# Hybrid streaming encoder layer: the mixing loop's tile in another order on all engines, and the pair diagonal by a product and a head mask

## What is computed

```python
def sink_attention(q, k, v, dist, valid, sinks):
    s = jnp.einsum('bnqkgd,bnskd->bnkgqs', q, k).astype(jnp.float32) * (HEAD_DIM ** -0.5)
    s = s - slopes[None, None, :, :, None, None] * dist[None, :, None, None, :, :]
    ...
    p = jax.nn.softmax(jnp.concatenate([s, sink], axis=-1), axis=-1)[..., :-1]
    return jnp.einsum('bnkgqs,bnskd->bnqkgd', p.astype(v.dtype), v)

def hgrn_block(S, q, k, i, logf):
    b = jnp.cumsum(logf, axis=1)
    decay = jnp.exp(jnp.where(causal, b[:, :, None] - b[:, None, :], -jnp.inf))
    a = jnp.sum(q[:, :, None] * k[:, None] * decay, axis=-1)
    o = jnp.einsum('btsh,bshv->bthv', a, i) + jnp.einsum('bthk,bhkv->bthv', q * jnp.exp(b), S)
    b_last = b[:, -1]
    kd = k * jnp.exp(b_last[:, None] - b)
    S_new = jnp.exp(b_last)[..., None] * S + jnp.einsum('bshk,bshv->bhkv', kd, i)
    return S_new, o

    ob = rmsnorm(ob, o_norm) * jax.nn.silu(gb)
    mix = jnp.concatenate([oa, ob], axis=-1)
    x = x + g1 * jnp.dot(mix, w_out)
    h2 = rmsnorm(x, ln2) * (1 + sc2) + sh2
```

## Time and profile before

| | |
|---|---|
| time, median of 3 runs (lowest to highest) | 1498.12 us (1497.85 to 1501.41) |
| the profiled execution's own time | 1499.57 us |
| its span in the trace | 1497.8 us |
| mean granted TensorE clock | 0.885 of full speed |
| PE busy | 1248.5 us, 83% of the span |
| DVE busy | 727.3 us, 49% |
| ACT busy | 547.4 us, 37% |
| POOL busy | 356.7 us, 24% |

### The profile page before, as it was taken

One profiled execution on the slowest core, in us unless ns is written; L12 is line 12 of the kernel. 1 busy time (PEld: TensorE's weight loads), 2 busy tenths in 40 slices (PEclk: granted clock), 3 DMA queues, 4 the chain that ended last, 5 costly groups with the idle time before them and its releaser, 6 DMA issues. The chain is left out here.

```text
span 1497.8 us, 21761 instructions
## 1 busy us (share of the span) xinstructions
PE 1248.5 (83%) x7145; PEld 1032.7 (69%) x7146; DVE 727.3 (49%) x1062; ACT 547.4 (37%) x921; POOL 356.7 (24%) x411
## 2 busy tenths in 40 slices
PE   4789999995285888888888882699999999969964
PEld 1668889884254777677777671588888787858853
DVE  2554313423343545644554526555338665865662
ACT  2454313322222334423433410444316544654540
POOL 1001100223202323332232200223143234323313
PEclk8899999998557978888889875799999999989988
DMA  9527653312806322212211105648757979888874
GB/s 344 209 78 267 228 199 104 106 43 75 223 1 177 98 68 95 81 44 67 96 44 57 38 32 216 219 154 266 241 167 246 357 252 303 282 304 260 267 279 84
DMA packets 119143, 249.89 MB, mean 167 GB/s; under 512 B 17681, under 2 KB 47121, under 8 KB 116002
## 3 DMA queue, kind: packets, MB, share of 16 engines
q1 hardware_dynamic: 106978, 204.92, 39.3%
q0 software_dynamic: 12096, 44.05, 11.2%
HBM read 205.02 MB, written 43.93 MB: 166 GB/s over the span
## 5 line engine op out<-in xcount | busy, mean ns | idle before, releaser
L2044 PE MATMUL psum<-e_w_h,e_x_h 128*128 128x512 f32 x432 | 174.3, 404 | 30.8 <-DVE w_gu L2157 23.9
L2045 PE MATMUL psum<-w_gu,e_x_h 128*128 x432 | 171.6, 397 | 0.0
L2046 PE MATMUL psum<-e_w_h,e_x_l 128*128 128x512 f32 x432 | 171.4, 397 | 0.0
L1991 POOL DMA_INDIRECT out<-e_work,e_to x26 | 87.9, 3379 | 302.9 <-DVE e_work L2145 302.9
L2157 DVE TENSOR_TENSOR w_gu<-w_gu,e_w_h 128x1024 f32 x128 | 146.7, 1218 | 21.4 <-ACT e_w_h L2098 21.4
L2098 ACT ACTIVATE e_w_h<-w_gu 128x1024 fp32r x128 | 123.0, 1048 | 53.6 <-issue 31.9
L2044 PEld LDWEIGHTS psum<-e_w_h,e_x_h 128*128 128x128 f32 x432 | 83.3, 193 | 49.2 <-DVE w_gu L2157 24.4
L465 PE MATMUL psum<-p_w_h,p_h_h 128*128 128x512 f32 (+1 forms) x288 | 106.4, 370 | 1.6 <-DVE p_h_l L620 1.6
L466 PE MATMUL psum<-p_w_l,p_h_h 128*128 128x512 f32 (+1 forms) x288 | 105.5, 366 | 0.0
L467 PE MATMUL psum<-p_w_h,p_h_l 128*128 128x512 f32 (+1 forms) x288 | 105.4, 366 | 0.0
L2046 PEld LDWEIGHTS psum<-e_w_h,e_x_l 128*128 128x128 f32 x432 | 83.1, 192 | 17.9
(11 more groups left out here) (362 smaller groups left out, 2647.9 us busy)
## 6 DMA issues: line engine op xcount, KB each, us to landing
w_gu<-in_w_e_gate SPq DMA_DIRECT2D x16, 2048.0 KB, 15.2
w_gu<-in_w_e_up SPq DMA_DIRECT2D x16, 2048.0 KB, 19.0
w_dn<-in_w_e_down SPq DMA_DIRECT2D x16, 2048.0 KB, 15.0
p_stage<-in_w_ada SPq DMA_DIRECT2D x24, 1024.0 KB, 6.6
p_w_raw<-in_w_in SPq DMA_DIRECT2D x5, 2048.0 KB, 9.2
m_feat<-feat_d SPq DMA_DIRECT2D x8, 1024.0 KB, 6.6
m_tok<-tok_d SPq DMA_DIRECT2D x8, 896.0 KB, 8.2
tok_d<-p_tok SPq DMA_DIRECT2D x27, 256.0 KB, 2.0
```

Of the source, the lines that this page charges most:

```text
L1991: pool.indirect_dma_start(out=d["y"], out_offset=bass.IndirectOffsetOnAxis(ap=to_now[1 - par][:, 0:1], axis=0), in_=y_s[:, 1 - par, :], in ...
L2044: pe.matmul(psum[:, j, :], x_h[:, k, :], wh, start=(k == 0), stop=False)
L2045: pe.matmul(psum[:, j, :], x_h[:, k, :], wl, start=False, stop=False)
L2046: last = pe.matmul(psum[:, j, :], x_l[:, k, :], wh, start=False, stop=(k == KC - 1))
```

## The change

- **The diagonal**: POOL multiplies K and Q element by element into a new tile `prod`, and PE sums it over the channels of each head by four matmuls against a mask of two columns (`head_cols`), which leave eight numbers a row in PSUM. DVE spreads these over the identity. The eight full products of 128 columns go.
- **The attention turn**: `o_a` is turned in the output bank W0, behind a wait for DVE's first step of `residual` (`x1_ready`), in place of S0.
- **The next query turn**: queries and keys of tile t + 1 are turned behind the last `fill` of tile t, ahead of the state update, and ACT copies them there (`keep_qk`). The diagonal of tile t + 1 stands between the state's part and the attention turn.
- **The order within a tile**: `scores` of the first half stands ahead of the first `fill`, two `fill`s stand between level 0 and level 1, the scores of the second half come ahead of level 3, and their `tops` on DVE ahead of `place` of level 3. On DVE `heads_normed` (the norm of group B's output), `normed` and `rest` of the second half go from where they were to behind a `place`. On ACT `norm` goes from the tile's end to behind `exp_b` of the next tile and uses `h2_t` as its scratch, and the copy of the attention turn goes ahead of the norm factors `o_rs`. On POOL the product stands ahead of the moves of `v`, then `k_d`, the third gap and `weigh`.

```diff
+        prod, head_cols = sb("prod", [P, QW]), sb("head_cols", [P, 2])
...
                 make_gap(t, 0)
                 make_gap(t, 1)
                 if t >= 1:
-                    pool.wait_ge(s["kd_turned"], t)
-                pool.tensor_tensor(f4(k_d[:, :]), f4(fts(t, EK)), last_bc(f4(fts(t, CUM))[:, :, P - 1:P], P), ALU.add).then_inc(s["kgap_ready"], 1)
-                if t >= 1:
-                    weigh(t - 1)
-                make_gap(t, 2)
+                    pool.wait_ge(s["diag_mm"], t)
+                else:
+                    pool.wait_ge(s["eps_made"], 1)
+                pool.tensor_tensor(prod[:, :], fts(t, KB), fts(t, QB), ALU.mult).then_inc(s["prod_ready"], 1)
                 pool.wait_ge(tok_loaded[t % 2], 16 * (t // 2 + 1))
                 if t >= 1:
                     pool.wait_ge(s["pv_mm"], 2 * t)
                     alone(pool)
...
-                else:
-                    pool.wait_ge(s["eps_made"], 1)
                 pool.tensor_copy(v_sb[:, 1, :], toks(t, TOK_V, KW)).then_inc(s["v_ready"], 1)
+                if t >= 1:
+                    pool.wait_ge(s["kd_turned"], t)
+                pool.tensor_tensor(f4(k_d[:, :]), f4(fts(t, EK)), last_bc(f4(fts(t, CUM))[:, :, P - 1:P], P), ALU.add).then_inc(s["kgap_ready"], 1)
+                make_gap(t, 2)
+                if t >= 1:
+                    weigh(t - 1)
...
-            for t in range(TP):
+
+            def turn_qk(t):
                 pe.wait_ge(tok_loaded[t % 2], 16 * (t // 2 + 1))
                 if t:
-                    pe.wait_ge(s["mixa_ready"], t)
+                    pe.wait_ge(s["pt_ready"], 2 * t)
...
                 last.then_inc(s["qk_turned"], 1)
-                pe.wait_ge(feat_loaded[t % 2], 16 * (t // 2 + 1))
-                pe.wait_ge(s["state_ready"], t + 1)
-                for h in range(8):
-                    r = slice((h % 2) * HD, (h % 2 + 1) * HD)
-                    c = slice((h // 2) * P, (h // 2 + 1) * P)
-                    last = pe.matmul(psum[:, M0 + h % 2, c], fts(t, KB)[r, c], fts(t, QB)[r, c], start=True, stop=True)
-                    if h >= 6:
-                        last.then_inc(s["diag_mm"], 1)
+
+            def diagonal(t):
+                pe.wait_ge(s["prod_ready"], t + 1)
+                for c in range(4):
+                    last = pe.matmul(psum[:, M0, 2 * c:2 * c + 2], prod[:, c * P:(c + 1) * P], head_cols[:, :], start=True, stop=True)
+                last.then_inc(s["diag_mm"], 1)
+
+            turn_qk(0)
+            diagonal(0)
+            for t in range(TP):
+                scores(t, 0)
                 fill(t, 0)
-                scores(t, 0)
                 level(t, 0)
+                fill(t, 1)
+                fill(t, 2)
+                level(t, 1)
+                turn_probs(t, 0)
+                fill(t, 3)
                 if t:
                     turn_ob(t - 1)
-                fill(t, 1)
-                level(t, 1)
+                level(t, 2)
                 if t:
                     pe.wait_ge(s["mixb_ready"], t)
                     turn_h2(t - 1)
-                fill(t, 2)
-                level(t, 2)
-                turn_probs(t, 0)
+                scores(t, 1)
+                level(t, 3)
                 if t:
                     logits(t - 1)
-                fill(t, 3)
+                fill(t, 4)
                 values(t, 0)
-                scores(t, 1)
-                level(t, 3)
-                fill(t, 4)
                 level(t, 4)
+                turn_probs(t, 1)
                 fill(t, 5)
-                turn_probs(t, 1)
                 level(t, 5)
                 fill(t, 6)
                 values(t, 1)
...
                 fill(t, 7)
+                if t + 1 < TP:
+                    turn_qk(t + 1)
...
+                pe.wait_ge(s["state_ready"], t + 1)
...
-                turn4(S0, o_a[:, :, :, :].rearrange("p g k d -> p (g k d)"), s["oa_turned"])
+                if t + 1 < TP:
+                    diagonal(t + 1)
+                pe.wait_ge(s["x1_ready"], t + 1)
+                turn4(W0, o_a[:, :, :, :].rearrange("p g k d -> p (g k d)"), s["oa_turned"])
...
-                a(score[:, :, :].rearrange("p g n -> p (g n)"), x2[:, u % 2, :], ACT.Square, accum_out=ss[:, :]).then_inc(s["squared"], 1)
+                if u < NU - 2:
+                    if u:
+                        act.wait_ge(s["logit_mm"], u)
+                        alone(act)
+                    out = h2_t[:, :, :].rearrange("p k r -> p (k r)")
+                else:
+                    out = score[:, :, :].rearrange("p g n -> p (g n)")
+                a(out, x2[:, u % 2, :], ACT.Square, accum_out=ss[:, :]).then_inc(s["squared"], 1)
...
+            def keep_qk(t):
...
-                gap_exp(t, 0)
+
+            act.wait_ge(s["eps_made"], 1)
+            high(0, 0)
+            high(0, 1)
+            gap_exp(0, 0)
+            gap_exp(0, 1)
+            keep_qk(0)
+            for t in range(TP):
...
-                gap_exp(t, 1)
+                if t:
+                    norm(t - 1)
+                gap_exp(t, 2)
+                act.wait_ge(s["kgap_ready"], t + 1)
+                a(k_d[:, :], k_d[:, :], ACT.Exp).then_inc(s["kexp_ready"], 1)
+                gap_exp(t, 3)
+                probs(t, 0)
+                copy_probs(t, 0)
+                gap_exp(t, 4)
                 if t:
                     keep_ob(t - 1)
                     high(t, 1)
-                act.wait_ge(s["kgap_ready"], t + 1)
-                a(k_d[:, :], k_d[:, :], ACT.Exp).then_inc(s["kexp_ready"], 1)
...
-                gap_exp(t, 3)
-                copy_probs(t, 0)
-                gap_exp(t, 4)
                 gap_exp(t, 5)
                 probs(t, 1)
                 gap_exp(t, 6)
                 copy_probs(t, 1)
+                if t + 1 < TP:
+                    gap_exp(t + 1, 0)
+                    gap_exp(t + 1, 1)
                 act.wait_ge(s["kd_turned"], t + 1)
                 a(kd_tok[:, :], psum[:, OB, :], ACT.Copy).then_inc(s["kdt_ready"], 1)
+                if t + 1 < TP:
+                    keep_qk(t + 1)
                 act.wait_ge(s["ob_mm"], t * 2 + 2)
                 a(o_sq.rearrange("p (a c) d -> p a (c d)", a=2), psum[:, OA:OA + 2, 0:4 * HD], ACT.Square).then_inc(s["osq_ready"], 1)
+                act.wait_ge(s["oa_turned"], t + 1)
+                a(mixed(t + 1, 0), f4(psum[:, W0, :]), ACT.Copy).then_inc(s["mixa_ready"], 1)
+                high(t + 1, 0)
                 act.wait_ge(s["oss_ready"], t + 1)
                 olink = Chain(act, s["o_rs"], 2 * t)
                 olink(a(o_rs[:, :], o_ss[:, :], ACT.Ln, scale=1.0 / HD, bias=eps[:, :]))
                 olink(a(o_rs[:, :], o_rs[:, :], ACT.Exp, scale=-0.5))
-                act.wait_ge(s["oa_turned"], t + 1)
-                a(mixed(t + 1, 0), f4(psum[:, S0, :]), ACT.Copy).then_inc(s["mixa_ready"], 1)
-                high(t + 1, 0)
-                norm(t)
+            norm(TP - 1)
...
+            for par in range(2):
+                dve.memset(head_cols[0:HD, par:par + 1], 1.0 - par)
+                dve.memset(head_cols[HD:P, par:par + 1], float(par))
...
-                decayed(t, 0)
-                dve.wait_ge(s["diag_mm"], t * 2 + 2)
-                if t:
-                    dve.wait_ge(s["ob_mm"], 2 * t)
-                    alone(dve)
-                dve.tensor_tensor(pair[:, :, :, :].rearrange("p a h t -> p (a h) t"), psum[:, M0:M0 + 2, :].rearrange("p a (h t) -> p (a h) t", t=P),
-                                  bc(ident[:, :], 1, 8), ALU.mult).then_inc(s["pair_clear"], 1)
-                decayed(t, 1)
-                if t:
-                    normed(t - 1)
-                tops(t, 0)
-                if t:
...
+            def heads_normed(t):
...
+            for t in range(TP):
+                decayed(t, 0)
+                dve.wait_ge(s["diag_mm"], t + 1)
+                if t:
+                    dve.wait_ge(s["ob_mm"], 2 * t)
+                    alone(dve)
+                dve.tensor_tensor(pair[:, :, :, :], last_bc(psum[:, M0, 0:8].rearrange("p (c a) -> p a c", a=2).unsqueeze(3), P),
+                                  bc(bc(ident[:, :], 1, 4), 1, 2), ALU.mult).then_inc(s["pair_clear"], 1)
+                decayed(t, 1)
+                tops(t, 0)
+                dve.wait_ge(s["pair_clear"], t + 1)
+                place(t, 0)
+                if t:
+                    heads_normed(t - 1)
+                decayed(t, 2)
+                place(t, 1)
+                if t:
+                    normed(t - 1)
+                denominators(t, 0)
+                decayed(t, 3)
+                place(t, 2)
+                if t:
+                    rest(t, 1)
+                decayed(t, 4)
+                tops(t, 1)
+                place(t, 3)
+                if t:
+                    keep_logits(t - 1)
...
+                place(t, 6)
+                residual(t)
+                dve.wait_ge(s["ob_mm"], 2 * t + 2)
```

(62 more changed lines are left out.)

11 lines of the change are left out of this document (added).

## The result

The changed kernel takes **1437.9 us** (median of four runs, 1432.15 to 1438.73) against 1497.98 for the kernel before: ratio 0.9592, 95% interval 0.9557 to 0.9627. It is faster, as forecast, by two thirds of the forecast 93 us, and 1.9 us above the range's upper end of 1436. The profiled execution took 1437.97 us, 61.6 less than that of before. Nearly all of it lies in the mixing loop: behind the last attention turn stand 619.2 us, before 620.3.

A forecast was written before the change was run, and what follows sets the result against it. PE was taken to bound the kernel through its work, its waits and a slow clock behind them. Gains of 10.9, 1.5, 11.4, 15.6, 3.1, 2.8 and 49.6 less 2.1 made 92.8 us: forecast 1405 us, range 1392 to 1436.

The forecast's parts named there:

- clock term: Tiles 1 to 7: without pauses of 2 us the slow clock behind them goes, gaining 49.6 us (35.7 to 57.5).
- The 13 busy microseconds at 1.00: Busy stretch at 636 to 649, logits and turns included, that kept full clock; cited against falls in busy work.
- The diagonal: Sixteen 128-column records become eight of two columns, 0.85 us in all; gain 0.35 us a tile, 2.8 us.
- The third rival: Slower: clock falls in the busy stretch between tiles without 512-column matmuls and stays low through fills; about 1607 us, chance 0.03.
- the second rival: Clock follows the kind of work, not the waits, and keeps falling; no clock gain, 1455 us, chance 0.05.
- The waits: PE's pauses in the mixing loop mostly go; 40.4 us gained with the tail's 1.5, three small waits remaining a tile.
- The tail: Behind the last tile, where no scores follow: wait falls from 3.69 to about 2.2 us, gaining 1.5.
- ahead of level 1: PE's wait for `place` of level 0: 0.4 us a tile left of 14.2 us in all, gaining 11.4.
- the first exponentials: PE's first probability turn waits for ACT: a new wait of 0.3 us a tile, costing 2.1 us.
- the first fill: Turn of the tile: PE waits 0.6 us for `rest` behind the scores, 15.1 us before, gaining 10.9.
- Moved waits: Other waits shifted by the new order, such as `x1_ready`, `ob_mm`, `norm` and the feature load: each costs zero.
- Tile 0: First tile's idle time of 6.0 us, 2.15 counted elsewhere; the other 3.8 become 0.7, gaining 3.1 us.

The follow-up runs named there:

- e7: Changed kernel with diagonal mask and logits both widened to 128 columns, and tile 0's first fill ahead of its diagonal and scores: 1405.1 us.
- e3: Changed kernel with the two-column diagonal mask read 64 times over, 128 columns a matmul, at the same place: 1421.7 us.
- e11: e7 with the two-column diagonal mask put back at its place, nothing else changed: 1432.2 us.
- e8: e7 with level 1 ahead of the third fill instead of behind it, so PE waits there again: 1426.8 us.
- e9: Changed kernel with the two-column diagonal mask read 16 times over, 32 columns a matmul: 1419.7 us.
- e12: e10 with the last fill's final matmul ahead of the pairs instead of behind three quarters of them: 1416.2 us.
- e10: e11 with the two-column diagonal moved ahead of the state update's matmuls and the last fill's six matmuls spread around it: 1431.2 us.

## Why the prediction was wrong, point by point

**The step that failed is the clock term**, "if pauses of 2 us go, what followed them goes", with "I found no fall in busy work". It was 49.6 us. Busy time of the loop fell by 12.9 in all, diagonal included, where the sum had 49.6 + 2.8 = 52.4. Tiles 1 to 7, on which the term was worked out, were 19.2 less busy (317.48 to 298.26), and tile 0 was 6.3 more. In e7, which but for the first fill of tile 0 keeps the changed kernel's order, and which has no falls in tiles 1 to 7, it fell by 354.4 - 302.4 = 52.0. So the size of the term was about right and its condition was not: the falls behind the waits went, and new ones came in busy work, at the turns. The 13 busy microseconds at 1.00 with the logits among them were no evidence against such falls: in e3 the clock goes right behind the logits in five tiles and stays in two.

**The diagonal** was costed by its records alone: 0.85 us forecast, 0.92 at 2.4 GHz in the second turn. The hidden price is 27.1 us on a kernel without other falls (e11 less e7) and about 16 in the changed kernel itself (after less e3, where the logits then lose the clock): the narrow diagonal thins out a stretch that was poor already. The third rival named this stretch, with the two-column diagonal in it. Its condition came true; its extent, low through all fills, did not: the clock was back after some 7 to 14 us, among the fills, so the cost was nowhere near 152. It was given 0.03, and no case stood for a part of it. The time lies between the forecast and the second rival (1455, no clock term at all), which was right in part too: the kind of work does make the clock fall, but waits do as well (e8).

**The waits** came out better than forecast: 47.8 us in the loop against 38.9 (40.4 less the tail's 1.5). With the clock at 1.00 they are what the sum said: 0.4 ahead of level 1, 0.3 at the first exponentials, 0.2 instead of 0.6 at the first fill, all in e7. In the changed kernel the slow work ahead of them hides them, worth 6.0 us (e7 less after), so this part of the gain is no merit of the new order. The tail gave 0.65 of its 1.5: 3.04 are left.

**Moved waits** at zero: right, no other line waits in the loop. **Tile 0**: its waits went, but it did not get the 3.1 us. Its busy time rose from 36.9 to 43.3 us; 1.7 of that is the next tile's query turn and diagonal, which now stand in it, and for the rest its turn, diagonal and scores started at the low clock and stayed there for 15.5 us from the first record (9.8 in e3, 15.8 in e11, 3.2 in e7, which has both the wide mask and the early fill).

Adding up: 47.8 of waits and 12.9 of busy time are 60.7 in the loop, with 1.1 behind it 61.8 of the 61.9 by which the span is shorter. That e7 lands on the 1405 of the forecast is no merit of the forecast: it needed edits that the change doesn't have.

## What to carry to other kernels

Do not cost a matmul by its time alone: where the clock follows what PE streams, saving columns in a stretch that is already thin can cost far more than it saves (here 16 to 27 us against a forecast 2.8), and reading the same operand several times over can be a gain. When waits are taken out, look at the busy stretches that are left and read the granted clock in each, on several tiles; one stretch at 1.00 proves nothing for the next tile (e3). A forecast that rests on the clock needs a case for a partial loss, not all or nothing.

## What had not been expected of the hardware

- The clock halves with PE busy every moment (513 to 521 of the kernel after), and the columns of four matmuls (eight records) in a tile of 39 us decide it (2: 1432.2 us; 128: 1405.1).
- A matmul's width was nearly free here: at 2.4 GHz the diagonal's eight records took 0.91 us to the next group with 2 columns (e11), 0.92 with 32 (e9) and 1.00 with 128 (e7).
- DVE's state update of 256 columns took 2.49 us beside POOL's `xw` in e12, where POOL had started 0.14 us earlier, and 0.42 in e10, where POOL started 0.27 later. The slow one ended 0.3 us after POOL did. The Trainium skill (SBUF — State Buffer, "SBUF: two separate sides") says that the two engines share a pair of ports as an exclusive lock, which the one that starts first keeps for a whole instruction; the trace agrees.
